# Eight early modulation chunks as padded matmuls over four output partition groups, with the first projection interleaved and the key/value projection two slots later

## What is computed

```python
def adaln_params(cond, w_mod, b_mod):
    m = jax.nn.silu(cond) @ w_mod + b_mod          # cond: 1024, w_mod: 1024 x 6144
    return jnp.split(m, 6, axis=-1)
...
# x (256 tokens) with its condition c, and a context xc (256 tokens) with c_ctx:
h   = rmsnorm(x,  g) * (1 + scale)     + shift
h_c = rmsnorm(xc, g) * (1 + scale_ctx) + shift_ctx
proj = h @ w_in                                     # queries, key/value, convolution and gates: 4352 columns
k_ctx, v_ctx = the key/value columns of h_c @ w_in  # 256 columns
```

## Time and profile before

| | us |
|---|---|
| median of 3 runs | 1578.48 |
| range of the runs | 1576.19 to 1580.05 |
| span of the profiled execution | 1577.9 |
| PE busy in it | 1413.4 (90%) |
| DVE busy | 1074.8 (68%) |
| ACT busy | 777.4 (49%) |
| POOL busy | 295.1 (19%) |

### The profile page before, as it was taken

The page is one execution under the profiler, slowest core; times in us unless marked ns, Lnnn a source line. Parts: engine busy times, 40 slices in busy tenths (PEclk is TensorE's granted clock), DMA queues, the critical chain, the costliest instruction groups (busy, mean ns, idle before and its releaser), DMA issues.

```text
span 1577.9 us, 21891 instructions
## 1 busy us (share of the span) xinstructions
PE 1413.4 (90%) x7816; PEld 1042.8 (66%) x7816; DVE 1074.8 (68%) x2270; ACT 777.4 (49%) x1649; POOL 295.1 (19%) x296
## 2 busy tenths in 40 slices
PE   7999988899998778778778889998999998999998
PEld 3889987544453223223222278998999987989997
DVE  4678665766666667766665578547777775477776
ACT  3655542444444444444444364746555566455555
POOL 0001100444454444434344300000000010000000
PEclk9999998999999999999999999999999999999999
DMA  9456755999999999999999944234555531245553
GB/s 398 177 204 224 249 175 211 372 418 427 427 426 427 427 427 426 427 426 427 427 427 426 428 186 154 106 108 161 183 175 179 182 127 61 94 167 184 188 186 130
DMA packets 62586, 432.91 MB, mean 274 GB/s; under 512 B 7073, under 2 KB 7585, under 8 KB 12193
## 3 DMA queue, kind: packets, MB, share of 16 engines
q0 software_dynamic: 41616, 285.76, 43.7%
q1 hardware_dynamic: 20160, 145.37, 26.0%
q10 hardware_dynamic: 720, 0.62, 0.1%
HBM read 430.67 MB, written 1.05 MB: 274 GB/s over the span
## 4 chain that ended last, share of the span: by engine, by line
PE 61%; DMA 19%; ACT 9%; DVE 8%; issue 2%; POOL 0%; ACTq 0%; DVEq 0%; POOLq 0%
PE banks L668 26%; PE banks L1059 15%; DMA arena<-in_peer_uv,experts 11%; DMA tok_b<-in_peer_uv,experts 4%; PE banks L1227 3%; PE banks L1195 3%; PE banks L705 3%; DVE wlow L1746 3%; ACT diag L1515 2%; PE banks L864 2%; PE banks L905 2%; PE banks L766 1%; ACT whigh L1271 1%; PE banks L824 1%; PE banks L845 1%
## 5 line engine op out<-in xcount | busy, mean ns | idle before, releaser
L1059 PE MATMUL banks<-arena,diag 128*128 128x512 f32 x780 | 382.9, 624 | 84.9 <-ACT diag L1515 84.9
L1746 DVE TENSOR_TENSOR wlow<-wring,whigh 128x1024 fp32r<-128x1024 f32 x234 | 276.0, 1221 | 121.5 <-ACT whigh L1271 121.4
L2190 DVE CUSTOM_DVE_ANT_0 arena<-arena,scores 128x1024 f32<-128x1024 f32 x200 | 245.2, 1226 | 162.5 <-DMA arena<-in_peer_uv,experts 160.5
L1059 PEld LDWEIGHTS banks<-arena,diag 128*128 128x128 f32 x780 | 140.2, 193 | 315.7 <-ACT diag L1515 191.5
L1271 ACT ACTIVATE whigh<-wring 128x1024 fp32r<-128x1024 f32 x234 | 234.6, 1050 | 97.6 <-DMA wring<-in_w_down 34.3
L1695 POOL DMA_INDIRECT arena<-in_peer_uv,experts x200 | 210.5, 1052 | 314.8 <-PE banks L1059 264.6
L668 PE MATMUL banks<-f_high,whigh 128*128 128x256 f32 x720 | 205.2, 285 | 8.0 <-DVE wlow L1746 5.5
L668 PE MATMUL banks<-f_low,whigh 128*128 128x256 f32 x720 | 203.7, 283 | 0.0
L668 PE MATMUL banks<-f_high,wlow 128*128 128x256 f32 x720 | 203.7, 283 | 0.0
L1507 ACT ACTIVATE dots<-dots 128x1 f32<-128x1 f32 x256 | 51.9, 203 | 302.3 <-DVE dots L2190 302.0
L668 PE MATMUL banks<-a_high,whigh 128*128 128x256 f32 x528 | 159.3, 302 | 11.8 <-DVE a_low L1792 6.0
(11 more groups left out here) (275 smaller groups left out, 2411.1 us busy)
## 6 DMA issues: line engine op xcount, KB each, us to landing
wring<-in_w_up SPq DMA_DIRECT2D x44, 1024.0 KB, 4.9
wring<-in_w_down SPq DMA_DIRECT2D x22, 1024.0 KB, 4.9
wring<-in_w_in SPq DMA_DIRECT2D x17, 1024.0 KB, 5.4
wring<-in_w_qkv_a SPq DMA_DIRECT2D x12, 1024.0 KB, 4.9
arena<-in_w_mod SPq DMA_DIRECT2D x8, 1024.0 KB, 15.6
arena<-in_w_mod_t POOLq DMA_DIRECT2D x16, 512.0 KB, 5.3
hT<-in_w_mod_t POOLq DMA_DIRECT2D x16, 512.0 KB, 4.7
wring<-in_peer_w_q SPq DMA_DIRECT2D x5, 1024.0 KB, 4.8
```

What stands on the lines that cost most here:

```text
L1059: mm = nc.tensor.matmul(banks[:, 2 + 2 * b + half, :], diag[:, n % DIAGS, :], ring[ROW_PLACE[n]][:, D + half * 512:D + (half + 1) * 512], ...
L1746: V.tensor_tensor(low, w, high.bitcast(F32), ALU.subtract).then_inc(w_split, 1)
L2190: V.tensor_tensor_reduce(out=ring[ROW_PLACE[n]][:, 0:D], in0=ring[ROW_PLACE[n]][:, 0:D], in1=h2tok[:, b, :], scale=1.0, scalar=0.0, op0=AL ...
```

## The change

- All eight chunks go through `mod_chunk`. `csil` is padded with zeros from 2 to 32 columns (cleared on POOL), and the eight k-tiles of a chunk write in turn to four groups of 32 output partitions (`QUADS`), so that each group adds up two of them. `rows_out` copies all 128 partitions. `mod_turn` is now a product with a constant that picks the two rows of each of the four groups and adds the groups up. The DVE way (`mod_by_rows`, `mod_columns`) is gone.
- The order is scale first (`MOD_ORDER` = 4, 5, 6, 7, 0, 1, 2, 3). The loads are x, chunks 4 to 7, the first ring chunk, chunks 0 to 3, the second, ctx, the third, c_row, constants. Ring order is 1, 2, 0 in place of 1, 0, 2.
- DVE scales hT as soon as the scale is there. The shift arrives chunk by chunk. For each pair of tiles ACT adds the shift and rounds in one instruction a tile (`round_shifted`), and DVE computes the low part as (scaled + shift) - high (`low_shifted`), two instructions a pair. hT itself no longer gets the shift. ACT starts the shift's `rows_out` when all eight tiles are scaled.
- The first projection is cut into four groups of 12 products (`first_projection`), one for each pair of tiles, placed between the last modulation chunks.
- The squares of the context are taken after the first projection's operands; DVE adds them up to two tiles (`add_squares`), and PE averages them with two products (`norm_sum_added`) in slot 3, in place of eight.
- `key_value` moves from slot 2 to slot 4, the rotation from slot 5 to 6, the duplication from 7 to 8, with the ACT and DVE steps that belong to them. c_row's Silu moves to after the context's rounding.

```diff
+MOD_ORDER = list(range(KT // 2, KT)) + list(range(KT // 2))
+QUADS, QUAD = 4, 32
...
-        csil = sb("csil", [P, KT, 2])
+        csil = sb("csil", [P, KT, QUAD])
...
+            sp.dma_start(xT[:, :, :].rearrange("p k t -> p (k t)"), a["x"]).then_inc(x_in, 16)
+            at = 0
+            for n, i in enumerate(MOD_ORDER):
+                if n == KT // 2:
+                    load(chunks[at]["slot"], chunks[at]["src"], chunks[at]["used"])
+                    at += 1
                 load_mod(i)
...
+            def mod_chunk(p):
+
+                pe.wait_ge(mod_in[MOD_ORDER[p]], 16)
+                if p >= 2:
+                    pe.wait_ge(mod_row_read, p - 1)
+                for k in range(KT):
+                    quad = slice(k % QUADS * QUAD, (k % QUADS + 1) * QUAD)
+                    mm = nc.tensor.matmul(banks[quad, 2 + p % 2, 0:WIDE], csil[:, k, :], mod_early[MOD_ORDER[p]][:, k, :],
+                                          start=(k < QUADS), stop=(k >= KT - QUADS))
+                mm.then_inc(mod_rows, 1)
+
             def mod_turn(p):
 
                 pe.wait_ge(mod_row_read, p + 1)
+                if p > KT // 2:
+                    pe.wait_ge(shift_ready, max(1, p - KT // 2 - 1))
                 for j in range(2):
-                    t = 2 * MODS_PE[p] + j
-                    mm = nc.tensor.transpose(banks[:, 7, 2 * t:2 * t + 2], mod_row[:, p % 2, j * P:(j + 1) * P],
-                                             ident[0:2, 0:2])
+                    t = 2 * MOD_ORDER[p] + j
+                    mm = nc.tensor.matmul(banks[:, mod_bank(p), 2 * t:2 * t + 2], mod_row[:, p % 2, j * P:(j + 1) * P],
+                                          const[:, C_QUADS:C_QUADS + 2], start=True, stop=True)
                 mm.then_inc(mod_made, 1)
...
+            def first_projection(g):
+
+                c = in_chunks[1]
+                for j in range(2):
+                    if g == 0:
+                        pe.wait_ge(w_split, 2 * c["split"] + j + 1)
+                    if j == 0:
+                        pe.wait_ge(h_ready, normed(0, 2 * g + 2))
+                    wh, wl = (t[:, c["slot"], :].rearrange("p (k n) -> p k n", k=KT)[:, :, j * P:(j + 1) * P]
+                              for t in (whigh, wlow))
+                    for k in (2 * g, 2 * g + 1):
+                        for n, (w, x) in enumerate(((wh, a_high), (wh, a_low), (wl, a_high))):
+                            mm = nc.tensor.matmul(banks[:, 0, j * T:(j + 1) * T], w[:, k, :], x[:, k, :],
...
             pe.wait_ge(cond_ready, 1)
+            for p in range(KT // 2):
+                mod_chunk(p)
+                if p == 0:
+                    pe.wait_ge(ident_in, 16)
+                else:
                     mod_turn(p - 1)
                 if p == 1:
                     norm_sum()
+            mod_turn(KT // 2 - 1)
+            for p in range(KT // 2, KT):
+                mod_chunk(p)
+                mod_turn(p)
+                if p > KT // 2:
+                    first_projection(p - KT // 2 - 1)
+            first_projection(3)
...
             for slot in range(plan["slots"]):
                 i, j = divmod(slot, 2)
-                if slot == 2:
+                if slot == 3:
+                    norm_sum_added(ctx_squares)
+                if slot == 4:
                     for which in range(2):
                         key_value(which, 0)
                         key_value(which, 1)
...
+            def round_shifted(k2, group, which, src, high):
+
+                for k in (2 * k2, 2 * k2 + 1):
+                    ins = nc.scalar.activation(high[:, k, :], src[:, k, :], ACT.Identity,
+                                               bias=mod[:, group * KT + k, which:which + 1])
+                ins.then_inc(h_rounded, 1)
...
+            square(xT, x_in, 16, step=0)
+            for p in range(KT // 2):
+                rows_out(p)
                 if p == 2:
                     act.wait_ge(ident_in, 16)
                     sqrt(0)
+            round_next()
+            act.wait_ge(scaled, KT)
+            for p in range(KT // 2, KT):
                 rows_out(p)
+                if p > KT // 2:
+                    act.wait_ge(shift_ready, p - KT // 2)
+                    round_shifted(p - KT // 2 - 1, 0, 0, hT, a_high)
+            act.wait_ge(shift_ready, KT // 2)
+            round_shifted(3, 0, 0, hT, a_high)
             round_next()
+            square(cT, ctx_in, 16, step=0, dst=ctx_squares)
+            round_next()
+            sqrt(1)
...
-            dve.wait_ge(cond_ready, 1)
-            mod_by_rows(0)
-            mod_by_rows(1)
             norm_inverse(0)
             low_next()
-            dve.wait_ge(mod_made, ROWS_1)
-            dve.wait_ge(mod_columns_made, len(MODS_DVE))
+            dve.wait_ge(mod_made, KT // 2)
...
+            step.link(modulation(KT, 2 * KT, 0))
             step.link(gains(0, 1, 0, V_N1))
             step.link(gains(1, 1, 1, V_N1))
+            scale(hT, xT, 0, gain1[:, 0, :], scaled)
+            for g in range(4):
+                dve.wait_ge(mod_made, KT // 2 + g + 1)
+                modulation(2 * g, 2 * g + 2, KT // 2 + g).then_inc(shift_ready, 1)
+                if g > 0:
+                    low_shifted(0, g - 1, 0, hT, a_high, a_low)
+            low_shifted(0, 3, 0, hT, a_high, a_low)
```

More of the change, by code:

```diff
@@ L113 @@
 C_IOTA = C_EPS + 1
-C_EARLY = C_IOTA + TOPK + 14
+C_QUADS = C_IOTA + TOPK
+C_EARLY = C_QUADS + 14
 C_ROT1 = C_EARLY
@@ L173, in shape_constants @@
     c[:, C_IOTA:C_IOTA + TOPK] = np.arange(TOPK)
+    for quad in range(QUADS):
+        c[quad * QUAD:quad * QUAD + 2, C_QUADS:C_QUADS + 2] = np.eye(2)
     return c
@@ L774, in mod_columns @@
[L774 to L780, removed]
-                        mm = nc.tensor.matmul(banks[:, 7, 2 * t + which:2 * t + which + 1],
-                                              mod_sum[:, n, which, j * P:(j + 1) * P], ones[:, 0:1], start=True,
-                                              stop=True)
-                mm.then_inc(mod_columns_made, 1)
@@ L1353, in shift @@
+            round_next()
+            sqrt(1)
+            for g in range(4):
+                act.wait_ge(scaled, KT + 2 * g + 2)
+                round_shifted(g, 0, 1, cT, c_high)
+            act.wait_ge(c_row_in, 16)
+            nc.scalar.activation(c_row, c_row, ACT.Silu).then_inc(c_row_ready, 1)
+            def shift(dst, count, group, which):
                 for k in range(KT):
                     act.wait_ge(scaled, count + k + 1)
-                    ins = nc.scalar.activation(dst[:, k, :], dst[:, k, :], ACT.Identity,
-                                               bias=mod[:, group * KT + k, which:which + 1])
@@ L1357, in shift @@
-                    ins.then_inc(shifted_x if high is not None else shifted, 1)
-                    if high is not None and k % 2:
-                        act.wait_ge(shifted_x, count + k + 1)
-                        copy(high[:, k - 1:k + 1, :], dst[:, k - 1:k + 1, :]).then_inc(h_rounded, 1)
-            def round_norm(count, src, high):
-                for g in range(4):
-                    act.wait_ge(scaled, count + 2 * g + 2)
-                    copy(high[:, 2 * g:2 * g + 2, :], src[:, 2 * g:2 * g + 2, :]).then_inc(h_rounded, 1)
@@ L1368, in _ @@
-            shift(hT, 0, 0, 0, a_high)
-            round_next()
-            sqrt(1)
-            shift(cT, KT, 0, 1, c_high)
-            round_next()
+                    nc.scalar.activation(dst[:, k, :], dst[:, k, :], ACT.Identity,
+                                         bias=mod[:, group * KT + k, which:which + 1]).then_inc(shifted, 1)
             dests = [(q1, 0), (q1, 1)]
@@ L1759, in norm_inverse, with scale @@
                 step.link(V.reciprocal(rstd[:, i % 2, :], root[:, i % 2, :]))
-            def scale(dst, src, i, gain, ready, pairs=None, norm=None):
-                def low(g):
-                    dve.wait_ge(h_rounded, normed(norm, 2 * g + 2))
-                    sl = slice(2 * g, 2 * g + 2)
-                    low_pair(pairs[1][:, sl, :], dst[:, sl, :], pairs[0][:, sl, :]).then_inc(h_ready, 1)
+            def scale(dst, src, i, gain, ready):
                 for k in range(KT):
@@ L1771, in scale, with low_shifted @@
                                            in1=rstd[:, i % 2, :], op0=ALU.mult, op1=ALU.mult).then_inc(ready, 1)
-                    if pairs is not None and k % 2 and k > 1:
-                        low(k // 2 - 1)
-                if pairs is not None:
-                    low(3)
+            def low_shifted(norm, g, which, src, high, low):
+                dve.wait_ge(h_rounded, normed(norm, 2 * g + 2))
+                for k in (2 * g, 2 * g + 1):
+                    ins = V.scalar_tensor_tensor(out=low[:, k, :], in0=src[:, k, :], scalar=mod[:, k, which:which + 1],
+                                                 in1=high[:, k, :].bitcast(F32), op0=ALU.add, op1=ALU.subtract)
```

(11 more changed lines are left out.)

138 lines of the change are left out of this document (46 added, 92 removed).

## The result

The changed kernel takes 1592.97 us (median; 1591.05 to 1599.12), the kernel before 1578.4: a ratio of **1.0095, with an interval of 1.0076 to 1.0113**. That is 14.5 us slower. I had forecast 1577.8 with a range to 1583.0. The profiled execution of the changed kernel has a span of 1589.7 us, 11.8 more than that of before.

The account below looks back on a forecast made before the run. PE was taken as the bound, busy 1413.4 of 1577.9 us. First projection ending at 51.6 instead of 53.2, plus 0.9 for the context's average, gave -0.7: span 1577.2, plus 0.6 to the median, 1577.8 us; range 1571 to 1583.

Parts of the forecast that it names:

- The price of a chunk: Modulation chunk on PE: 1.0 us at full clock, 2.0 at half, if the four output groups overlap; 3.5 if not.
- The loads: Opening: scale chunks land at 9.0, 11.6, 14.3 and 17.0 us; loads bind only at the first four chunks.
- The start at half clock: Opening up to scaled hT: PE's first work at half speed, norm_sum 4.8 us, scaling done at 30.4 us.
- The round trips: First projection: after each of three chunks, 2.5 us of copy, turn, rounding and low parts, then 12 products.
- The clock in them: PE enters the round trips at half clock; full clock returns in the second or third round, 21.2 us in all.
- T: The end of the first projection, where the edit ends: forecast 51.6 us, against 53.2 in the kernel before.
- half clock to the end: Rival, round trips: clock stays at half, +2.4 us, or +3.5 with a late opening, 1581 to 1582; chance 0.12.
- What was hidden: After T: context chain hides with 0.6 us to spare; PE has no idle time from there through key_value.
- the average: Context's average moved onto PE's path in slot 3, two products in place of eight: 0.9 us added.
- Passing through after T: After T order and releasers are the same, so the opening's shift should reach the end of the kernel.
- T of before: End of the first projection in the kernel before: 53.2 us, from SP's ring load issued at 53.38.
- The sum: Whole kernel: 51.6 - 53.2 + 0.9 = -0.7 us, span 1577.2, median 1577.8 us.

Follow-up runs that it names:

- e7: e2 with all eight k-tiles of a chunk in one group of 32 output partitions: 1592.58 us, ratio 1.0091.
- e6: e2 without the round trips: shift rows copied out as they come, the 48 products in one piece: 1570.05 us, ratio 0.9936.
- e5: e2 with unused products that keep PE busy in the round trips: 1578.07 us, ratio 0.999.
- e3: The changed kernel with 192 bytes more of unused space behind csil, 1152 above the kernel before: 1595.55 us, ratio 1.0094.
- e11: The changed kernel itself, measured again beside e9 and e10 on one chip: 1594.08 us, ratio 1.0066.
- e2: The changed kernel with 64 bytes more of unused space behind csil, 1024 above the kernel before: 1582.38 us, ratio 1.002.
- e8: The kernel before with 26 unused products ahead of the first projection: 1586.95 us, ratio 1.0047.
- e1: The kernel before with only csil's allocation widened, moving everything behind it by 960 bytes: 1592.58 us, ratio 1.0066.
- e4: The kernel before with 128 bytes more of unused space: 1589.66 us, ratio 1.0048.
- e10: The kernel before with 64 bytes more of unused space: 1593.09 us, ratio 1.0051.
- e9: The kernel before with 256 bytes more of unused space: 1580.86 us, ratio 0.9991.
- e12: e6 with one unused product after each shift chunk and three ahead of the first projection: 1570.92 us, ratio 0.9924.

## Why the prediction was wrong, point by point

- **The price of a chunk** (1.0 and 2.0): right, 1.04 and 1.93. The 1.09 from the earlier trace rows was slightly cautious. By the rule of the Trainium skill, "TensorE: Matmul & The Clock Gate", Part 3, that loads overlap only when the row groups differ, the groups would have run one after the other. They share all rows and do overlap here, so the measurement (1.04, against 3.57 in e7) decides against that reading, and the page's 2.38 for three groups is of the same kind as the 3.4 for four.
- **The loads**: chunk 5 forecast at 11.6, PE starts on it at 12.11. Right to half a microsecond. The last shift chunk landed in time in the changed kernel and becomes the bound in e6.
- **The start at half clock**: too short. I gave `norm_sum` 4.8 us, taking the 3.3 us of slow work from the earlier trace rows. There PE worked without a pause from 9.1. Here it has to stop for a load between the first two chunks, and `norm_sum` took 6.48 in the changed kernel and 5.38 in e5. In e7, where PE works without a pause from 9.28 to 18, it took 3.65. That the pause is the cause is still only argued. The scaling ended at 32.67, not 30.4, outside my bounds of 28.4 to 31.5.
- **The round trips**: their steps were right within 0.1 us each (copy 0.39, shift and round 0.89, low part 0.87), 2.6 us between chunk and products where I had 2.5. But the wait is not the one I wrote down. The turn (1.02 at half clock) and DVE's bias run beside ACT's pair and end after it, so the low part waits for them (timeline):

```profile
36.36 0.89 ACT L1356 ACTIVATE a_high<-hT,mod 128x256 fp32r<-128x256 f32 x2
37.57 0.16 DVE L1826 TENSOR_TENSOR mod<-banks,vcol 128x4 f32<-128x4 f32 x1 [3.22 <-PE banks L776]
```

  In e5, at full clock, the same turn takes 0.49 in the chain and the whole step 2.3.
- **The clock in them**: wrong. I expected it back in the second or third round. It stayed at 1.2 GHz through all of them in the changed kernel and in e3 and e11, T 58.66 to 58.9. In e2's execution it came back for parts and T was 53.8. Both happened with PE busy for about two thirds of the time (20.15 of 30 us in the changed kernel, 16.18 of 25 in e2). My rival "half clock to the end" (T = 54.7) was the right mechanism, but it too was 4.0 us short: 2.3 from the later scaling, and 1.65 from the products, which took 2.90 + 2.93 + 5.32 = 11.15 where I had 9.5.
- **What was hidden**: right. From 58.66 PE has no gap through slots 2 to 5 (2.87, 0.86 and 23.02 us without a break); `key_value`, the context's chain and the new queue order cost nothing, and the average costs 0.86 for 0.9 forecast.
- **Passing through after T**: right for what the opening gains or loses (e8, e6), with 2 to 3 us of scatter from 200 to 280 us.
- **T of before**: I took SP's issue at 53.38 to come 0.2 after T. In the changed kernel, e5 and e6 it comes 0.03 to 0.04 after, so T was 53.3, and the sum should have read -0.8.
- **The sum**: the opening was forecast at -0.7 and is worth +3 (interval -0.3 to +6.8, e2). On the 1578.4 of before that is 1581.6, still in the range. Of the 15.2 us by which 1592.97 misses the forecast, this is 3.8. **The step that failed was that "after T the order and releasers are the same, so the shift should pass through to the end"**, taken to mean that nothing else changes. I costed the padding of `csil` by the clearing on POOL alone. The change added 960 bytes in front of every buffer that the gathers write, and that is worth 8 to 10 us (e1, e4, e3 against e2, e10 against e9): the gathers take 649.2 to 651.8 us in place of 639.5 to 642.1, over all 14 profiled executions. Neither a rival nor the range had room for a stage 220 us behind the edit.

**Left open.** Where the 256-byte effect arises no run tells, and places between the steps of 64 bytes were not tried. All three profiled executions with this opening on a slow place have T at 58.7 to 58.9, and the one on the fast place (e2) has 53.8. They differ before the round trips already: `norm_sum` takes 6.47 to 6.53 in those three and 5.09 to 5.96 in e2, e5, e6 and e12, which have the same opening up to there on the fast place. Whether the place has a part in that, or chance, isn't separated, so the split into 10 us of address and 3 us of opening could also be read as 9 and 6 (the rate, and the 6.14 at slot 9), which gives 15. Nor do I know why the TensorE clock after the gathers differs between executions of the same instructions. Before has 0.94 and 0.97 in 1280 to 1400, e5's execution 0.86 and 0.85 over the same instructions. After the last gather e5 needs 666.7 us and before 657.8, so 9 us of its profiled span came after the part that was edited. Over all 14 profiled executions this last part takes 655.2 (e9) to 666.7, with fast and slow places mixed. It is the largest scatter in these times, and it is why the rate and the length of the gathers say more than one whole time does.

## What to carry to other kernels

A tile that grows moves everything allocated behind it. Ask of every size change which later buffers shift, by how much modulo 256 bytes, and whether a DMA-bound stage writes them. A few floats of padding settle it: here 64 bytes took the changed kernel from a ratio of 1.0095 to 1.002. And a chain that hops between engines can be paid twice: here the gaps also kept TensorE at 1.2 GHz. When one engine's step is made short, put its instances together and hop once (e6) instead of hopping once for each.

## What the runs showed of the hardware

- Gathers of 8 KB rows ran at 427 or 421 GB/s, going by where the tiles behind `csil`, their destinations among them, lay within 256 bytes (shifts of 0, 256 and 1024 bytes against 64, 128, 960 and 1152).
- Plain loads that kept the DMA engines busy (12 to 32 us) showed the same: 424 to 426 GB/s against 419 to 421.
- Float32 products of 512 columns on four groups of output partitions ran 3.4 times as fast as in one (1.04 against 3.57 us for the same 16 records), with all rows of the array shared.
- In the changed kernel the granted clock stayed at 1.2 GHz for 30 us while PE was busy for 20.15 of them. With twelve unused products after the first shift chunk and three more in each later round it stayed at 2.4 GHz (e5).
